# A state-space stage in rounds: outputs before the next tile's lag products, and the lag products in a bank of their own, copied late among the powers of B

## The reference

```python
def s5_scan(u, lam_bar, b_bar, s0, reverse):
    bu = jnp.einsum('btgh,gph->btgp', u, b_bar)
    ...
    _, states = lax.associative_scan(_lin_rec_combine, (a, bu), axis=1, reverse=reverse)
    return states
...
        st_lat = s5_scan(uc_lat, lam_bar, b_bar, s_ctx_final, reverse)
        y_lat = y_lat + jnp.einsum('btgp,ghp->btgh', st_lat, c_mat).real
```

## Time and profile before

| | |
|---|---|
| device time, three runs | 3556.96, 3558.69, 3559.35 us; median 3558.69 |
| the profiled execution | 3554.54 us, of which 3552.7 us is the span from first to last instruction |
| busy share of the span | PE 92%, PEld 78%, DVE 60%, ACT 39%, POOL 14% |
| mean granted TensorE clock | 0.955 of full |
| chain that ended last | PE 83%, DVE 6%, POOL 5%, issue 2%, DMA 2% |

### The profile page before, as it was taken

The page is one execution under the profiler, slowest core; times in us unless marked ns, Lnnn a source line. Parts: engine busy times, 40 slices in busy tenths (PEclk is TensorE's granted clock), DMA queues, the critical chain, the costliest instruction groups (busy, mean ns, idle before and its releaser), DMA issues.

```text
span 3552.7 us, 51801 instructions
## 1 busy us (share of the span) xinstructions
PE 3286.0 (92%) x21097; PEld 2763.3 (78%) x21097; DVE 2145.0 (60%) x1850; ACT 1380.7 (39%) x1385; POOL 480.5 (14%) x352
## 2 busy tenths in 40 slices
PE   5788899799999999886789999999999899999998
PEld 3445578688888888675678888888868788888887
DVE  7668755565555555699565555555644555555555
ACT  4446543433333333322234434433323344344332
POOL 2869900000000000096000000000000000000000
PEclk7888899899999999998799999999999999999999
DMA  9988875255555555344145555555524455555552
GB/s 299 305 282 257 260 243 175 91 184 189 185 189 182 190 186 189 107 142 148 36 154 178 186 190 182 186 189 189 177 92 142 142 186 184 187 187 189 189 183 89
DMA packets 351014, 643.22 MB, mean 181 GB/s; under 512 B 21599, under 2 KB 50359, under 8 KB 350519
## 3 DMA queue, kind: packets, MB, share of 16 engines
q1 hardware_dynamic: 309952, 561.68, 48.9%
q10 hardware_dynamic: 40951, 79.98, 6.6%
HBM read 637.54 MB, written 4.06 MB: 181 GB/s over the span
## 4 chain that ended last, share of the span: by engine, by line
PE 83%; DVE 6%; POOL 5%; issue 2%; DMA 2%; ACT 1%; SPq 1%; DVEq 1%; ACTq 0%; POOLq 0%
PE acc L439 49%; PE acc L440 25%; POOL cpow L1841 3%; DMA raw<-in_w_mod_dram 2%; POOL ptmp L1841 1%; PE acc L1263 1%; DVE z L943 1%; DVE w_lo L793 1%; PE acc L1280 1%; PE acc L521 1%; PE acc L533 1%; PE acc L464 1%; PE acc L1188 1%; PE acc L1247 1%; DVE hf L832 0%
## 5 line engine op out<-in xcount | busy, mean ns | idle before, releaser
L439 PE MATMUL acc<-xin,w_hi 128*128 128x512 f32 x5376 | 1915.2, 399 | 58.9 <-DVE xin L807 33.7
L793 DVE TENSOR_TENSOR w_lo<-raw,w_hi 128x2048 fp32r<-128x2048 f32 x484 | 1111.2, 2301 | 1079.0 <-ACT w_hi L640 1078.8
L440 PE MATMUL acc<-xin,w_lo 128*128 128x256 f32 x5376 | 1519.4, 283 | 0.0
L640 ACT ACTIVATE w_hi<-raw 128x2048 fp32r<-128x2048 f32 x484 | 926.8, 1917 | 1365.1 <-PE acc L440 1365.0
L439 PEld LDWEIGHTS acc<-xin,w_hi 128*128 128x128 f32 x5376 | 1017.2, 189 | 312.5 <-issue 35.6
L440 PEld LDWEIGHTS acc<-xin,w_lo 128*128 128x128 f32 x5376 | 1021.5, 190 | 0.0
L439 PE MATMUL acc<-hid,w_hi 128*128 128x512 f32 x2432 | 845.4, 392 | 0.0
L440 PE MATMUL acc<-hid,w_lo 128*128 128x256 f32 x2432 | 681.2, 280 | 0.0
L439 PEld LDWEIGHTS acc<-hid,w_hi 128*128 128x128 f32 x2432 | 455.1, 187 | 101.4
L440 PEld LDWEIGHTS acc<-hid,w_lo 128*128 128x128 f32 x2432 | 459.6, 189 | 0.0
L799 DVE TENSOR_REDUCE tmp<-acc 128x1024 f32<-128x2048 f32 x116 | 265.0, 2284 | 19.9 <-PE acc L440 19.9
(11 more groups left out here) (241 smaller groups left out, 2063.5 us busy)
## 6 DMA issues: line engine op xcount, KB each, us to landing
raw<-in_ffn_w_gate_dram SPq DMA_DIRECT2D x88, 1024.0 KB, 5.2
raw<-in_ffn_w_up_dram SPq DMA_DIRECT2D x88, 1024.0 KB, 5.1
raw<-in_ffn_w_down_dram SPq DMA_DIRECT2D x88, 1024.0 KB, 5.1
raw<-in_w_mod_dram ACTq DMA_DIRECT2D x76, 1024.0 KB, 9.7
raw<-in_w_mlp_in_dram SPq DMA_DIRECT2D x64, 1024.0 KB, 5.2
raw<-in_w_mlp_out_dram SPq DMA_DIRECT2D x64, 1024.0 KB, 5.1
raw<-in_s_w_glu_dram SPq DMA_DIRECT2D x32, 1024.0 KB, 5.3
raw<-in_ab_w_in_dram SPq DMA_DIRECT2D x32, 1024.0 KB, 5.3
```

What stands on the lines that cost most here:

```text
L439: pe.matmul(bank, w_hi[:, slot, w], operand[:, kt, :], start=(kt == 0), stop=False)
L440: ins = pe.matmul(bank[:, 0:TOK], w_lo[:, slot, w], operand[:, kt, 0:TOK], start=False, stop=(kt == UK * units - 1))
L640: act.activation(w_hi[:, slot, :], raw[:, slot, :, :].rearrange("p k n -> p (k n)"), ACT.Copy).then_inc(hi_ready, 1)
L793: dve.tensor_tensor(w_lo[:, slot, :], raw[:, slot, :, :].rearrange("p k n -> p (k n)"), w_hi[:, slot, :].bitcast(F32), SUB).then_inc(lo_re ...
```

## The change

- PE's round k becomes `outputs(k)`, `lag_blocks(k+1)`, `states(k+1)`, and then as before.
- The lag products go to columns 0 to 239 of bank 7 in place of bank 5. `lag_blocks` no longer waits for `lpp_sb` and `e_sb`; it waits for the copy of the tile before and for `finish` of the tile two before. `output_transposes(n)`, which writes the other half of bank 7, now waits for `copy_lags(n+1)`.
- DVE's round k becomes `rotate(k)`, `finish(k-1)`, ten of the twelve operations of `powers_of_b(k+2)`, `copy_lags(k+1)`, the last two operations, `modulation`. 

No instruction is added or removed.

```diff
             def lag_blocks(n, b):
                 pe.wait_ge(cpow_done, n + 1)
                 pe.wait_ge(bd_sb, n + 1)
-                pe.wait_ge(lpp_sb, min(n + 2, KT))
-                pe.wait_ge(e_sb, 4 * (n + 1))
+                if n == 0:
+                    pe.wait_ge(par_sb, 1)
+                else:
+                    pe.wait_ge(r_sb, n)
+                if n > 1:
+                    pe.wait_ge(z_lo, n - 1)
...
-                            ins = pe.matmul(ps[5][32 * kp:32 * kp + 32, to:to + P],
+                            ins = pe.matmul(ps[7][32 * kp:32 * kp + 32, to:to + P],
...
             def output_transposes(n):
                 pe.wait_ge(y_gelu, n + 1)
+                pe.wait_ge(r_sb, min(n + 2, KT))
...
             for k in range(-1, KT):
+                if k >= 0:
+                    outputs(k, k % 2)
                 if k + 1 < KT:
                     lag_blocks(k + 1, (k + 1) % 2)
                     states(k + 1, (k + 1) % 2)
-                if k >= 0:
-                    outputs(k, k % 2)
...
-            def powers_of_b(c, n):
+            def powers_of_b(c, n, between=None):
...
                 c(tt(o[1][0], o[1][0], t, SUB))
                 c.settle()
+                if between is not None:
+                    between()
                 c(tt(t, pw[1][1], bv[1][0], MUL))
...
             for k in range(KT):
                 rotate(c0, k, k % 2)
-                if k + 1 < KT:
-                    copy_lags(c0, k + 1)
                 if k:
                     finish(k - 1)
+                if k + 2 < KT:
+                    dve.wait_ge(s_done, k + 1)
+                    powers_of_b(c0, k + 2, lambda: copy_lags(c0, k + 1))
+                elif k + 1 < KT:
+                    copy_lags(c0, k + 1)
                 if k in (0, 3, 5):
                     modulation(cm, {0: 1, 3: 2, 5: 3}[k])
-                if k + 2 < KT:
-                    dve.wait_ge(s_done, k + 1)
-                    powers_of_b(c0, k + 2)
```

More of the change, by code:

```diff
@@ L1716, in copy_lags @@
                     dve.wait_ge(r_out, 16 * n)
-                c(dve.tensor_copy(rw[:, 0:7 * GRP], ps[5][:, 0:7 * GRP]))
-                c(dve.tensor_copy(rw[:, 8 * GRP:15 * GRP], ps[5][:, 8 * GRP:15 * GRP]))
-                dve.scalar_tensor_tensor(rw[:, 7 * GRP:8 * GRP], eye, par[:, n + cols["s5_d"]:n + cols["s5_d"] + 1], ps[5][:, 7 * GRP:8 * GRP],
+                c(dve.tensor_copy(rw[:, 0:7 * GRP], ps[7][:, 0:7 * GRP]))
+                c(dve.tensor_copy(rw[:, 8 * GRP:15 * GRP], ps[7][:, 8 * GRP:15 * GRP]))
+                dve.scalar_tensor_tensor(rw[:, 7 * GRP:8 * GRP], eye, par[:, n + cols["s5_d"]:n + cols["s5_d"] + 1], ps[7][:, 7 * GRP:8 * GRP],
                                          MUL, ADD).then_inc(r_sb, 1)
```

## The result

| | before | after |
|---|---|---|
| median | 3558.49 us (8 runs, 3556.28 to 3560.69) | 3570.32 us (8 runs, 3567.91 to 3585.90) |
| ratio | | 1.0039, 95% interval 1.0025 to 1.0052 |
| span of the profiled execution | 3552.7 | 3566.1 |
| first product of the matrix layers (L439) starts at | 465.07 | 473.13 |

The change made the kernel slower. The medians differ by 11.8 us (0.33%), where 15.8 were forecast; the ratio, taken over all runs, is 1.0039, since two of the eight runs after took 3577.57 and 3585.90 us. Of the 13.4 us by which the two spans differ, 8.1 are there when the matrix layers begin; the rest came in these unchanged layers. The median less the L439 time was 3086 to 3098 us over the fourteen kernels of this study, so a few microseconds of either sign there mean nothing.

The account below looks back on a forecast made before the run. POOL in series with PE was taken to bound the stage at 20.6 us a round. Ten rounds of 22.2 plus 17.6, less 221.1 and 2.7, gave +15.8 us, a median of 3574.5; range 3545 to 3596.

Parts of the forecast that it names:

- C: Length of a steady round in the new order, 4.6 us plus the DRAM round trip: forecast 22.2, break-even 20.6.
- a last round: The round to outputs(15), without new weights: 4.6 + 13.0 = 17.6 us.
- Outputs first: Early rounds: outputs(1) fills PE's hole before 139.56, and the gain is kept: −2.7 us (bounds 0 and −2.8).
- What comes in its place: PE's outputs(k+1) waits for lags back from DRAM within one round: 4.6 us plus round trip, between 17.6 and 26.2.
- Which T: T, from the lag write's issue to the last read's landing: 5.7 + 3.8 + 8.1 = 17.6 us.
- second rival: Gain and loss cancel: T of 15.4 to 16.7, rounds 20.0 to 21.3 us, 3558.7 within 7 us; chance 0.18.
- Late copy on DVE: copy_lags behind ten operations of powers_of_b costs 0; about 1 us if the round were 20.
- The other signs: If right: outputs waits for DMA, rounds near 22 us, POOL idle about 3, L1247 not waiting for POOL, outputs(1) before 139.5.
- The bank and the waits: output_transposes waiting for copy_lags, the changed waits of lag_blocks and DVE's new order: 0.
- Clock: PE idles some 4.5 us before outputs, so the lower clock may fall there: taken as 0.
- the range's case: Outputs and lag products at the lower clock, states at the full one: +2 us a round, kept for the range.
- The first rival: Transfers hidden and POOL the bound: rounds of 19.2 us, −14.2 us, 3544.5; chance 0.22.

Follow-up runs that it names:

- Kernel 4: Changed kernel with PE's outputs first only from round 5 on, the old order before: 3563.22 us, 1.0019 against the kernel before.
- kernels 5 to 7: Tile 0's Toeplitz blocks for all tiles: changed kernel, transfers kept; changed kernel, later transfers dropped; kernel before, later transfers dropped: 3545.37, 3534.94, 3542.42 us.
- kernel 3: Changed kernel with the lag copy behind four instead of ten operations of the powers of B: 3572.22 us, 1.0038 against the kernel before.
- kernel 8: Changed kernel with outputs' Toeplitz term, and the wait for the transfers, behind its four state terms: 3559.16 us, 1.0005 against the kernel before.
- Kernel 1: Changed kernel with PE's old order, bank 7 and the late copy kept: 3558.02 us, 1.0002 against the kernel before.
- kernel 5: Changed kernel, outputs using tile 0's Toeplitz blocks for every tile, so no later wait; write and reads still made: 3545.37 us, 0.9969 against before.

## Why the prediction was right, and where it was not

The direction stands, and so does the cause: the round trip through DRAM, which the new order put on the path. The size is luck. In the prediction's own terms, new minus old is ten rounds of C, a last round, less 221.1 and the shift: forecast 222 + 17.6 − 221.1 − 2.7 = 15.8; measured 206.3 (236.99 to 443.27) + 16.1 − 221.1 + 6.5 = 7.8, half of it. The ten rounds of C were over by 15.7 us and the last round by 1.5, and the shift was under by 9.2. The 11.8 of the medians lies nearer to the forecast because the layers behind added some 4 us, which is within their spread.

*Outputs first, the shift of −2.7: wrong in sign.* Measured +6.5 (236.99 against 230.51). The step said that the hole before tile 2's lag products would take `outputs(1)`. It did not reckon that tile 0 already has the closed loop (9.01 us of wait, outputs at the lower clock), which moved the weights' transfers by 3.5 us before that hole, nor that the round trip would lengthen the weight transfers that bind these rounds. Kernel 4 gives the part as 7.1 us in the median and 6.4 at round 4, kernels 5 to 7 its cause. With the steady rounds at break-even, this term is nearly the whole of the stage's loss.

*What comes in its place, the closed loop: right that a loop through DRAM binds, but it is not the one described for most of the stage.* The loop within one round is on the chain at tile 0, tile 5 and tile 15, in the long rounds of kernel 3 and from tile 10 on in kernel 8. The early rounds between go over the weights. In the changed kernel, from tile 8 to tile 14, the loop goes over two rounds, through the powers of Λ and B and the late copy. Kernel 1 shows that the order of PE's work makes the loss, and kernels 5, 6 and 8 that the wait, the traffic and what stands behind the wait are its parts.

*Which T: mis-sized.* I gave every round T = 17.6: 5.7 for the write and 11.9 for the reads. Ten writes took 1.7 to 5.3 us, 2.5 in the middle:

```profile
DMA to landing us min/median/max: 1.7/2.5/5.3
```

In the four long rounds T was 13.9 to 15.5: 1.8 to 5.4 for the write and 10.2 to 12.1 for the reads. So the reads were sized right and the write was not. In the short rounds T was hidden behind PE's own work. So C was 20.6 over the ten rounds, where 22.2 was forecast: at break-even, and within the bounds of the second rival, gain and loss cancel. In kernels 3 and 8, where the write comes sooner, T is 17.8 to 19.3 and 16.9 to 17.3 in the long rounds, and there the forecast term is met. In the last round T was at most 9.4 (449.93 to 459.37), not 13.0, with outputs at the lower clock.

*Late copy on DVE, 0: wrong in every second round.* The working was right as far as it went: it put the copy 25.0 us behind the start of outputs, and it started 25.1 behind (321.84 to 346.93). But it was held against C = 22.2 for all rounds, with 1 us at C = 20. Rounds that alternate weren't among my cases; behind a round of 17.3 us the copy is 4.0 late. This is the sign of being wrong that the prediction named, a copy over 1 us late, and the reading it gave for it, that DVE's order is then the bound, holds only in part: taking the lateness away (3) won nothing, for the transfers take it back.

*The other signs.* `outputs` did wait for the transfers, and L1251 (L1247 before) no longer waits for POOL. Rounds near 22 us came only every second time, POOL idled 3 us in the short rounds and 0.4 in the long ones, and `outputs(1)` did not come before 139.5 but at 141.14.

*The bank and the waits, 0: right* (kernel 1). *Clock:* outputs did run at the lower clock in long rounds (granted 0.50 from 360 to 366), 4.7 us for 2.8, and the states behind them at the full one, 2.1 for 3.4, as the range's case had it.

*The first rival*, POOL as the bound at 19.2, is what the kernel does when the round trip is left out: 19.29. The rule weighed beside it stands in the Trainium skill (DMA: Bandwidth & Descriptors, "Queues, rings and completion order"): each DMA engine takes turns between the queues that have work, a packet at a time. The prediction's estimate from it, that small reads take no more than about twice their quiet time, would have made T 13.7. In the changed kernel the last read of the long round, issued at 354.36 beside the burst, took 7.2 us, where 4.2 is twice the quiet time, so the trace doesn't bear out that estimate here either. The measured T lies nearer to 13.7 than to 17.6, but only because the write was short.

What stays open: why the write took 5.4 us in one long round and 1.8 in another, why kernel 5 gained 25 us in the median and 13.8 at L439, and how much of the 3.8 us between the loss at L439 and the median's is more than spread.

## What to carry to other kernels

When an operation is moved ahead of another on a queue, write down the loop that closes: how many rounds of slack a transfer through DRAM had, and what now stands behind it each round. A gain in a series of engines can be real (7.5 us here without the transfers) and still be lost to it. Then take from behind the transfer what needn't stand there: the term order inside one accumulation was worth some 10 us in the new order and nothing in the old. Look also for loops over two rounds: a leg that is harmless behind an average round can bind behind a short one. And reckon the first rounds and the end of the stage by themselves, where other bounds rule.

## What the runs showed of the hardware

The same 120 KB write took 9.3 us to the first read in the kernel before, issued at 336.02 behind two loads of x (334.59 and 335.21), while the DMA engines were full until 342 (share 1.05 to 1.07), and 2.1 us after (327.84 to 329.94), issued with no load just ahead of it, as the burst ended (0.89 from 326 to 328, 0.20 in the next 2 us). Which of the two, the loads ahead or the burst, made the difference isn't separated. Either way the length of a transfer hangs on when it is issued, by as much as 7 us here. And the alternation of 17 to 18 us and 22 to 23 us held for seven rounds without damping, a pattern that a mean over rounds hides.
